# Weight buffers moved to multiples of 2048 bytes, moving tiles left 128 bytes past one

## The reference

```python
h = modulate(rmsnorm(x, norm_g[l, 0]), sh1, sc1)
x = x + 0.5 * g1[:, None, :] * swiglu(h, w_ffn1_in[l], w_ffn1_out[l])
h = modulate(rmsnorm(x, norm_g[l, 1]), sh2, sc2)
hq, hf_f, hf_b, hi, hg, aq, ak, av = split_columns(h @ w_mix_in[l])
o_hgrn = hgrn2_group(hq, hf_f, hf_b, hi, hg, lb_all[:, l], hgrn_norm_g[l])
o_attn = windowed_gqa(aq, ak, av, qk_norm_g[l, 0], qk_norm_g[l, 1], attn_sink[l], rel_bias)
mixed = jnp.concatenate([o_hgrn, o_attn], axis=-1) @ w_mix_out[l]
x = x + g2[:, None, :] * mixed
h = modulate(rmsnorm(x, norm_g[l, 2]), sh3, sc3)
x = x + 0.5 * g3[:, None, :] * swiglu(h, w_ffn2_in[l], w_ffn2_out[l])
```

## Time and profile before

| | |
|---|---|
| median of three runs | 1063.24 us |
| span of the profiled execution, first to last instruction | 1061.2 us |
| PE busy | 1042.3 us (98%) |
| PE weight load busy (beside PE) | 861.2 us (81%) |
| DVE busy | 589.4 us (56%) |
| ACT busy | 395.8 us (37%) |
| POOL busy | 48.8 us (5%) |
| moved by DMA | 133.50 MB, 126 GB/s over the span |

### The profile page before, as it was taken

How to read it: one execution, slowest core, us unless ns; L and a number is a source line. 1 busy time by engine, 2 the same in 40 slices (tenths; PEclk the granted TensorE clock), 3 DMA queues, 4 the chain that set the end, 5 groups by cost and what they waited for, 6 DMA issues and landing times.

```text
span 1061.2 us, 12566 instructions
## 1 busy us (share of the span) xinstructions
PE 1042.3 (98%) x5028; PEld 861.2 (81%) x5028; DVE 589.4 (56%) x674; ACT 395.8 (37%) x438; POOL 48.8 (5%) x33
## 2 busy tenths in 40 slices
PE   5999999999999999999999999999999999999998
PEld 3788888888888888888888898888888888888886
DVE  6896564554745689467788549873222232333323
ACT  4644242322323255363535773452121212223231
POOL 0000000000000060010200000510000000000000
PEclk9999999999999999999999999999999999999999
DMA  9667646555445422422120031313323223232312
GB/s 326 237 214 277 222 159 211 185 188 209 159 172 224 163 80 80 112 87 80 41 70 30 2 80 41 117 42 120 119 79 112 85 93 104 80 119 79 119 40 79
DMA packets 93739, 133.50 MB, mean 126 GB/s; under 512 B 10722, under 2 KB 77150, under 8 KB 93575
## 3 DMA queue, kind: packets, MB, share of 16 engines
q1 hardware_dynamic: 93374, 130.83, 36.4%
q10 hardware_dynamic: 328, 2.17, 0.5%
HBM read 130.88 MB, written 4.21 MB: 127 GB/s over the span
## 4 chain that ended last, share of the span: by engine, by line
PE 94%; DVE 3%; DMA 1%; ACT 1%; issue 1%; SPq 0%; DVEq 0%; ACTq 0%
PE bank L1745 26%; PE bank L1747 26%; PE bank L1746 26%; PE bank L2071 2%; PE bank L2180 2%; PE bank L2273 1%; PE bank L2166 1%; PE bank L1893 1%; PE bank L1879 1%; PE bank L1885 1%; PE bank L2155 1%; DMA x_nat<-in_x 1%; PE bank L1830 1%; PE bank L2256 1%; DVE tmod L1177 1%
## 5 line engine op out<-in xcount | busy, mean ns | idle before, releaser
L1745 PE MATMUL bank<-h_hi,w_hi 128*128 128x512 f32 x880 | 345.6, 393 | 0.1
L1747 PE MATMUL bank<-h_hi,w_lo 128*128 128x512 f32 x880 | 342.6, 389 | 0.0
L1746 PE MATMUL bank<-h_lo,w_hi 128*128 128x512 f32 x880 | 342.5, 389 | 0.0
L1103 DVE TENSOR_TENSOR w_lo<-w_raw,w_hi 128x2048 fp32r<-128x2048 f32 x81 | 186.5, 2302 | 276.9 <-ACT w_hi L675 276.8
L675 ACT ACTIVATE w_hi<-w_raw 128x2048 fp32r<-128x2048 f32 x81 | 155.2, 1916 | 490.4 <-PE bank L1747 485.2
L1745 PEld LDWEIGHTS bank<-h_hi,w_hi 128*128 128x128 f32 x880 | 165.2, 188 | 36.5 <-issue 2.1
L1747 PEld LDWEIGHTS bank<-h_hi,w_lo 128*128 128x128 f32 x880 | 165.1, 188 | 34.8
L1746 PEld LDWEIGHTS bank<-h_lo,w_hi 128*128 128x128 f32 x880 | 165.2, 188 | 33.9 <-issue 0.5
L1745 PE MATMUL bank<-a_hi,w_hi 128*128 128x512 f32 x352 | 137.6, 391 | 0.0
L1747 PE MATMUL bank<-a_hi,w_lo 128*128 128x512 f32 x352 | 137.0, 389 | 0.0
L1746 PE MATMUL bank<-a_lo,w_hi 128*128 128x512 f32 x352 | 137.0, 389 | 0.0
(11 more groups left out here) (270 smaller groups left out, 951.1 us busy)
## 6 DMA issues: line engine op xcount, KB each, us to landing
w_raw<-in_w_ffn_in SPq DMA_DIRECT2D x42, 1024.0 KB, 5.1
ada<-in_w_ada SPq DMA_DIRECT2D x28, 1024.0 KB, 5.0
w_raw<-in_w_ffn_out SPq DMA_DIRECT2D x22, 1024.0 KB, 4.8
w_raw<-in_w_mix_in SPq DMA_DIRECT2D x11, 1024.0 KB, 5.1
shift_in<-in_w_ada SPq DMA_DIRECT2D x4, 1024.0 KB, 8.7
scale_in<-in_w_ada SPq DMA_DIRECT2D x4, 512.0 KB, 7.6
x_nat<-in_x SPq DMA_DIRECT2D x2, 1024.0 KB, 8.8
scale_half<-in_w_ada SPq DMA_DIRECT2D x2, 1024.0 KB, 11.4
```

The lines of the kernel that those rows point to most:

```text
L1103: ve.tensor_tensor(w_lo[n % 2][:], src[:], as_f32(w_hi[n % 2][:]), ALU.subtract).then_inc(wlo_done, 1)
L1745: te.matmul(out_ap, wh, xh, start=first, stop=False)
L1746: te.matmul(out_ap, wh, xl, start=False, stop=False)
L1747: return te.matmul(out_ap, wl, xh, start=False, stop=last)
```

## The change

No instruction is added, removed or reordered on any engine, and no size or wait changes; only addresses do. Three small tiles, `masks` (1024 bytes), `softmax_stats` (640) and `lb_t` (256), are taken before the weight buffers instead of after them. Together they have 1920 bytes, and 128 + 1920 = 2048, so `w_raw` now begins at 67,584, a multiple of 2048, and with it `w_hi`, `w_lo` and `o_ada`. What is laid over these buffers moves with them: the four `bias` tiles, `scale_acc` and `quarter_acc` (over `w_raw`), and `ada`, `ada_acc`, `a_diag`, `av`, `tot_f`, `tot_b`, two of the `v_nat`, `o_sq`, `rto`, `table`, one `scale_half` and two `shift_in` (over `o_ada`). `ident` and `ones` also move up by 1920 bytes, to 0 and 512 past a multiple of 2048; `vec` and the small tiles up to `ind_r` by 896 bytes, the next ones by 640. From `warm` on nothing moves, since the sum of sizes is the same: `sel_b` and the whole `region` keep their addresses, as do `xT`, `h_hi` and `h_lo`.

```diff
     h_lo = at("h_lo", [P, DT, TOK], f32r, o_lo)
+    masks = at("masks", [P, LEVELS, P], mybir.dt.uint8, take(1024))
+    st = at("softmax_stats", [P, 5, 32], f32, take(640))
+    lb_t = at("lb_t", [P, 8, 8], f32, take(256))
     O_RAW0, O_RAW1 = take(8 * KB), take(8 * KB)
+    assert O_RAW0 % 2048 == 0
     raw = [at(f"w_raw{s}", [P, 2048], f32, o) for s, o in enumerate((O_RAW0, O_RAW1))]
@@
     ones = at("ones", [P, P], f32, take(512))
-    masks = at("masks", [P, LEVELS, P], mybir.dt.uint8, take(1024))
     vec = at("vec", [P, P], f32, take(512))
@@
     ind_r = at("ind_r", [P, 18], f32r, take(72))
-    lb_t = at("lb_t", [P, 8, 8], f32, take(256))
     lbv, omlb = lb_t[:, 6, :], lb_t[:, 7, :]
@@
     relb = at("relb", [NB + 1, QH], f32, take(32))
-    st = at("softmax_stats", [P, 5, 32], f32, take(640))
     warm = at("warm", [P, 3], f32, take(12))
```

## The result

| | before | after |
|---|---|---|
| median | 1063.22 us (4 runs) | 1084.01 us (4 runs, 1083.22 to 1084.67) |
| ratio | | 1.0193, 95% interval 1.0181 to 1.0206 |
| span of the profiled execution | 1061.2 us | 1082.9 us |
| PE busy | 1042.3 us | 1064.2 us |

What follows compares the result with a forecast made beforehand. The prediction took PE's unbroken row of matmuls, 226.6 ns each, to bound the kernel. Four terms of 0 left the span at 1061.2 us; with 2.0 us for the runs' median, 1063.2 us, range 1053 to 1076 us.

Steps and rivals of the forecast that it cites:

- What bounds the kernel: Whole span: a row of matmuls without holes; 3984 at 226.6 ns make 903 us, 85% of the span.
- terms two to four: ACT and DVE on moved buffers, loads into `w_raw`, small tiles and overlays: 0 us each.
- the first term: Stationary operand of the 3984 matmuls, slices now at multiples of 512: 0 ns, bounds -46 us to +22 us.
- the weak point of the 10 rows: Matmuls with `sel_a` and `sel_b`, used as guide to the full ones, have 10 rows instead of 128.
- The argument on periods: Slices at offsets 0 to 1536 run at one rate; a distance conflict must repeat every 256 or 512 bytes.
- The rival on the slower side: Every stage: equal offsets keep the read streams in step; parted, up to 5.6 ns per matmul, 1085 us; chance 0.12.
- The rival on the faster side: Every stage: 13.3 ns are a read conflict from equal offsets, which the change parts; 1017 us in full; chance 0.13.
- rival (c): Start only: loads and the norm's chain land sooner or later, 2 to 4 us, 1060 or 1066 us; chance 0.07.
- The prediction's estimate: Loads into `w_raw`: 32 beats instead of 36 per piece at an aligned offset, 4.5 instead of 5.1 us per load.

Runs made afterwards that it cites:

- e1_rest_only: Kernel before with the overlays on `o_ada`, `ident`, `ones` and small tiles moved as in the change, weight buffers unmoved: 1063.17 us, ratio 0.9998.
- s1_64_128: Kernel before with 64 bytes taken before `h_hi` and 64 before `w_raw`; distance 64 for `h`, 128 for `a`: 1086.76 us.
- c32_before: Kernel before with 32 instead of 128 weight columns in all but the first and last product of an accumulation: 1079.93 us.
- s2_256_192: Kernel before with 448 bytes taken before `h_hi` and 256 before `w_raw`; distance 256 for `h`, 192 for `a`: 1065.01 us.
- s8_all_256: Kernel before with 256 bytes taken before `w_raw`, so the distance is 256 in every stage: 1063.42 us, ratio 0.9998.
- e3_both_at_0: Kernel before with `h_hi`, `h_lo` and weight buffers at multiples of 2048, `region` tiles still at 128 past one: 1070.38 us, ratio 1.0064.
- e2_weights_only: Kernel before with only `w_raw`, `w_hi` and `w_lo` moved to multiples of 2048: 1084.7 us, ratio 1.0197.
- s6_32_224: Kernel before with 192 bytes taken before `h_hi`, 64 before `w_raw`, weights 32 bytes earlier; distance 32 for `h`, 224 for `a`: 1086.44 us.
- e4_low_only: Kernel before with only `w_lo` moved to a multiple of 2048, `w_hi` left at 128 past one: 1079.66 us.
- s5_each_its_own: Kernel before with `h_hi` and `w_hi` at phase 128 modulo 256, `h_lo` and `w_lo` at 192: 1079.57 us.
- s4_hlo64: Kernel before with `h_lo` at 192 past a multiple of 2048, weights at 640; distance 0 for `h_hi` and `a`, 448 for `h_lo`: 1075.97 us.

## Why the prediction was wrong

**What bounds the kernel**: right. The matmuls' step is the time, and all of the change shows in it. The terms two to four held: `e1_rest_only` puts the overlays on `o_ada` and the constants at 0 within 0.1%, and the start did not move.

**The step that failed** is the first term, "I take 0 ns", and in it the reading of two kinds of rows. I took 232 ns as the ordinary step beside them and concluded that neither load nor offset matters to a matmul. Measured, the term is 5.7 to 6.7 ns per matmul, some 21 us.

The matmuls with `ind_r` do not stand behind an interruption, as the prediction says. The 15 steps before the first of them are an even (516.73 - 513.33) / 15 = 226.7 ns:

```profile
513.33 0.39 PE L1745 MATMUL bank<-h_hi,w_hi 128*128 128x512 f32 x1
```

With `ind_r` the steps go up at once, to 232 ns. Its slices are 10 columns wide and begin 64 to 96 bytes past the start of their moving tile modulo 256. Either may be the reason: `s1_64_128` has 233.3 ns at 64, and `c32_before` 231.1 ns with a short load. So the row that was read as "leaves the step as it is" had the loss in it: it had to be compared with the 226.7 ns right before it, not with the 232 ns of ordinary matmuls elsewhere.

The matmuls with `sel_a` and `sel_b` do stand behind an interruption, and there ordinary matmuls at the good distance go at 232 ns as well. So they compare, with each other, steps that are not down at 226.7 ns, whatever their distance. That `sel_b` stands at d = 384 modulo 512, just as the changed weights do, was right, but its single step of 230 ns is given to 10 ns, and 5.7 ns were asked for the earlier trace rows. The text named the weak point of the 10 rows and then took the value all the same.

What the runs show in place of "0 ns": 226.7 ns was found only with one common phase modulo 256 and a full load, and 229 to 233 ns in all other long stretches.

**The argument on periods** was half right. It said that a conflict blind to steps of 512 must have a period of 256 or 512, and used that against the conflict. The period is 256 (`s2_256_192`, `s8_all_256`). A regularity that the rows did not exclude was no evidence against it.

**The rival on the slower side** had the place and the price: every stage, 5.6 ns per matmul, 1085 us; measured 5.7 to 6.7 ns and 1084.0 us. Of its mechanism, "no longer settles" is not what the trace shows: the steps settle as soon as before, on a slower pattern. It got a chance of 0.12 for one observation that spoke for it, that the rate settles over some ten matmuls at all. That observation pointed the right way. Its second half, that equal offsets are what gives the fast step, is shown by `e3_both_at_0`. The range ended at 1076 us, inside this rival's own price.

**The rival on the faster side**: no distance gave less than 226.7 ns (0, 32, 64, 128, 192, 224, 256, 320, 384 and 448 were tried), so at none of these placements do the 13.3 ns over the columns go away. That part of the reasoning stands. On the sentence of the Trainium skill on the load's own read port (TensorE: Matmul & The Clock Gate, "Step-by-step: what each phase is for"): that a load does not take read bandwidth from the running matmul agrees with this much: parting the two reads won nothing. It must not be read as if placement were free: in `e2_weights_only` it costs 21.5 us. Whether bandwidth is what is lost there no run shows; that a quarter of the reads does not bring the step down (`c32_before`) speaks against it.

**The loads**: rival (c) was right that a load to an aligned offset lands sooner and that this isn't seen in the time; the start did not move by the 2 to 4 us that it had. `w_raw` lands in 4.9 us after the change, in 5.1 before; it is 4.9 in every kernel that has it at a multiple of 256 bytes (`s1_64_128` among them) and 5.1 in every other (`s8_all_256`), a gain of 4%. The prediction's estimate from the Trainium skill (DMA: Bandwidth & Descriptors, "How a descriptor splits into AXI transactions") was 12%. The rows are of after (`s1_64_128` has the same) and of `s8_all_256`:

```profile
w_raw<-in_w_ffn_in SPq DMA_DIRECT2D x42, 1024.0 KB, 4.9
```
```profile
w_raw<-in_w_ffn_in SPq DMA_DIRECT2D x42, 1024.0 KB, 5.1
```

## What to carry to other kernels

In a kernel that is a row of fp32r matmuls, with a new 128-column slice for each, give the stationary and moving tiles that take turns the same start modulo 256 bytes, and check it again when a constant is added ahead of a buffer: 32 bytes cost 2% here (`s6_32_224`). Other matmul types were not tried, and the plain float32 matmuls of this kernel kept their 216 ns. Read the start-to-start step over some hundred matmuls in an unbroken stretch; neither the length of the records nor a single step shows 6 ns. And a row that is to stand for another must be in the same state as that one: compare it with the steps right before it, and remember that steps right behind an interruption say nothing on a settled stream.

## What the runs showed that I had not expected

The step over a long stretch, by distance modulo 256 bytes, with the two moving tiles in one phase and all weight buffers in one:

| d | 0 | 32 | 64 | 128 | 192 | 224 |
|---|---|---|---|---|---|---|
| ns | 226.7 | 233.3 | 233.3 | 232.4 to 233.3 | 228.9 | 233.3 |
| in units of 13.33 ns | 17 | 17.5 | 17.5 | 17.43 to 17.5 | 17.17 | 17.5 |

13.33 ns are 32 cycles at 2.4 GHz, in which a stream reads 128 bytes. At d = 0 every step is 17 such units; elsewhere the steps form a repeating pattern that closes on a whole number of them: 35 in two steps, 52 in three (`e4_low_only` and `s5_each_its_own`, 231.1 ns), 103 in six, 122 in seven, 261 in fifteen (`s4_hlo64`). At d = 128 two patterns occur with the same distance (232.4 and 233.3 ns in the changed kernel's two stretches; which one comes is not decided by the distance). The simple reading, that a stream waits for its turn in a rotation of 13.33 ns, failed in `s4_hlo64`. What rotates, if anything does, and why less than a full load gives a slower pattern, stays open. No version beat the kernel before.
